# Down projections of a three-term float32r kernel: one 512-column product for the high weights instead of two of 256 columns

## The reference, cut to what matters

```python
# first block (tag f1 in the kernel), weights w_up / w_down
u = causal_depthwise_conv(h2 @ w_up[l], w_conv[l], b_conv[l])
val, gte = jnp.split(u, 2, axis=-1)
x = x + (1 + gate2[:, None, :]) * ((val * jax.nn.silu(gte)) @ w_down[l])
...
# second block, layer a (f2: a_gu / a_down) and layer b (f3: b_gu / b_down)
def swiglu(h, w_gu, w_down):
    gate, up = jnp.split(h @ w_gu, 2, axis=-1)
    return (jax.nn.silu(gate) * up) @ w_down
x = x + swiglu(rms_norm_2(x, a_norm2_g[i]), a_ffn_gu[i], a_ffn_down[i])
...
return rms_norm_2(x, final_norm_g)
```

## Time and profile before

| what | value |
|---|---|
| median of the three runs | 1055.43 us |
| lowest and highest | 1054.33 and 1056.28 us |
| span of the profiled execution | 1051.3 us |
| mean granted clock of TensorE in it | 0.997 of full speed |
| busy: PE, PEld, DVE, ACT | 97%, 92%, 70%, 53% |

### The profile page before, as it was taken

How to read it: one execution, slowest core, us unless ns; L and a number is a source line. 1 busy time by engine, 2 the same in 40 slices (tenths; PEclk the granted TensorE clock), 3 DMA queues, 4 the chain that set the end, 5 groups by cost and what they waited for, 6 DMA issues and landing times.

```text
span 1051.3 us, 22984 instructions
## 1 busy us (share of the span) xinstructions
PE 1020.2 (97%) x10004; PEld 966.9 (92%) x10004; DVE 733.6 (70%) x1194; ACT 562.0 (53%) x858; POOL 0.9 (0%) x7
## 2 busy tenths in 40 slices
PE   7999999999999999998999999999999999999996
PEld 6898889999999998986879999999888799999996
DVE  3898677899976667888557566566857665565654
ACT  4456474665565548764236444454667654444541
POOL 0000000000000000000000000000000000000000
PEclk9999999999999999999999999999999999999999
DMA  9978465466645553331005555465224435554541
GB/s 350 398 259 310 172 239 186 176 239 242 229 139 193 203 231 121 126 118 43 4 6 196 199 174 190 140 214 209 101 78 166 170 124 201 191 175 158 194 166 41
DMA packets 31236, 185.82 MB, mean 177 GB/s; under 512 B 3472, under 2 KB 4768, under 8 KB 13984
## 3 DMA queue, kind: packets, MB, share of 16 engines
q1 hardware_dynamic: 31136, 184.36, 49.2%
HBM read 183.29 MB, written 1.05 MB: 175 GB/s over the span
## 4 chain that ended last, share of the span: by engine, by line
PE 87%; DVE 5%; DMA 3%; ACT 3%; issue 1%; SPq 1%; DVEq 0%; ACTq 0%
PE banks L383 47%; PE banks L1390 17%; PE banks L348 3%; PE banks L380 2%; PE banks L660 1%; DMA land<-in_mkv_a 1%; DVE wlo L328 1%; PE banks L1933 1%; PE banks L1574 1%; PE banks L595 1%; PE banks L1923 1%; ACT whi L313 1%; PE banks L663 1%; DMA raw<-in_a_in 1%; DMA raw<-in_w_in 1%
## 5 line engine op out<-in xcount | busy, mean ns | idle before, releaser
L328 DVE TENSOR_TENSOR wlo<-raw,whi 128x2048 fp32r<-128x2048 f32 (+3 forms) x163 | 323.0, 1982 | 169.3 <-ACT whi L313 169.1
L313 ACT ACTIVATE whi<-raw 128x2048 fp32r<-128x2048 f32 (+3 forms) x163 | 270.7, 1663 | 107.4 <-PE banks L1390 73.5
L383 PE MATMUL banks<-h_lo,whi 128*128 128x256 f32 x1376 | 175.1, 279 | 0.0
L383 PE MATMUL banks<-h_hi,wlo 128*128 128x256 f32 x1376 | 173.1, 277 | 0.0
L383 PE MATMUL banks<-h_hi,whi 128*128 128x256 f32 x1360 | 172.1, 279 | 0.1
L383 PEld LDWEIGHTS banks<-h_lo,whi 128*128 128x128 f32 x1376 | 163.9, 187 | 3.2 <-issue 2.6
L383 PEld LDWEIGHTS banks<-h_hi,wlo 128*128 128x128 f32 x1376 | 163.8, 187 | 1.5 <-issue 1.2
L383 PEld LDWEIGHTS banks<-h_hi,whi 128*128 128x128 f32 x1360 | 162.1, 187 | 2.3 <-issue 1.2
L1416 ACT ACTIVATE u<-u 128x256 f32<-128x256 f32 x44 | 18.4, 418 | 124.9 <-DVE u L1470 124.9
L1390 PE MATMUL banks<-m_lo,whi 128*128 128x256 f32 x528 | 73.4, 278 | 0.0
L1390 PE MATMUL banks<-m_hi,wlo 128*128 128x256 f32 x528 | 73.2, 277 | 0.0
(11 more groups left out here) (453 smaller groups left out, 1408.8 us busy)
## 6 DMA issues: line engine op xcount, KB each, us to landing
raw<-in_ada SPq DMA_DIRECT2D x24, 1024.0 KB, 6.6
raw<-in_w_up SPq DMA_DIRECT2D x22, 1024.0 KB, 4.8
raw<-in_a_gu SPq DMA_DIRECT2D x22, 1024.0 KB, 4.8
raw<-in_b_gu SPq DMA_DIRECT2D x22, 1024.0 KB, 4.9
raw<-in_w_in SPq DMA_DIRECT2D x12, 1024.0 KB, 6.4
raw<-in_w_down SPq DMA_DIRECT2D x16, 704.0 KB, 4.1
raw<-in_a_in SPq DMA_DIRECT2D x11, 1024.0 KB, 6.3
raw<-in_a_down SPq DMA_DIRECT2D x16, 704.0 KB, 4.1
```

Source lines behind the costliest of these rows:

```text
L313: act.activation(hi_s[k % NSPLIT][:, 0:w], raw[n % NRAW][:, 0:w], ACT.Copy).then_inc(*hi_made.tick(k))
L328: dve.tensor_tensor(lo_s[s][:, 0:w], raw[n % NRAW][:, 0:w], hi_s[s][:, 0:w].bitcast(F), SUB).then_inc(*lo_made.tick(k))
L383: i_ = pe.matmul(b[0:m, j * T:(j + 1) * T], a[:, kt * step + j * m:kt * step + j * m + m], x[:, kt, :], start=st, stop=sp)
```

## The change

The gated values get one buffer `gated` of two halves, `m_hi` and `m_lo`, in place of two buffers. For f = 0 to 6 the terms with `whi` are no longer two matmuls of 256 columns: one matmul of 512 columns reads the `m_hi` and the `m_lo` tile of a block and writes both halves of the bank, one per input part. After each one follows the `wlo` matmul of 256 columns for the same block. So one f is 44 matmuls instead of 66, with the same 22 x 768 columns. For f = 7 the order and the shapes stay as they were. In the first half of f = 0 the matmul of a block now also waits for `m_lo`, and in the second half it waits for it two matmuls earlier than before. DVE has to add the second half of the bank: one more scalar_tensor_tensor per f in f1, a copy and an addition more per f in f2 and f3.

```diff
-        m_hi = sb("m_hi", [P, 22, T], R, s2)
-        m_lo = sb("m_lo", [P, 22, T], R, s2)
+        gated = sb("gated", [P, 2, 22, T], R, s2)
+        m_hi, m_lo = gated[:, 0, :, :], gated[:, 1, :, :]
...
-                    if f == 0 and half == 1:
-                        turns = [(n, kt) for kt in range(11) for n in range(3)]
+                    if f == 0:
+                        turns = [(n, kt) for kt in range(11) for n in range(2)]
+                    elif f < 7:
+                        turns = [(n, kt) for kt in range(11) for n in range(2)]
                     else:
                         turns = [(n, kt) for n in range(3) for kt in range(11)]
                     for o, (n, kt) in enumerate(turns):
-                        a, x = (lo if n == 1 else hi), (m_lo if n == 2 else m_hi)
+                        g = 11 * half + kt
+                        w = (lo if n == 1 else hi)[:, kt * P:kt * P + P]
                         if n == 1:
                             pe.wait_ge(*lo_made.at(k))
                         if f == 0 and n == 0:
-                            pe.wait_ge(*m_hi_a.at((tag, 11 * half + kt)))
-                        if f == 0 and n == 2:
-                            pe.wait_ge(*m_lo_v.at((tag, 11 * half + kt)))
+                            pe.wait_ge(*m_hi_a.at((tag, g)))
+                            pe.wait_ge(*m_lo_v.at((tag, g)))
                         last = o == len(turns) - 1
-                        x_ = pe.matmul(b[:, 0:T], a[:, kt * P:kt * P + P], x[:, 11 * half + kt, :],
-                                       start=half == 0 and o == 0, stop=half == 1 and last)
+                        st, sp = half == 0 and o == 0, half == 1 and last
+                        if f < 7 and n == 0:
+                            x_ = pe.matmul(v2(b), w, gated[:, :, g, :], start=st, stop=False)
+                        else:
+                            x_ = pe.matmul(b[:, 0:T], w, (m_lo if n == 2 else m_hi)[:, g, :], start=st, stop=sp)
...
                 if up == "w_up":
+                    if f < 7:
+                        dve.scalar_tensor_tensor(out=X[:, f, :], in0=b[:, T:2 * T], scalar=GATE2[:, f:f + 1],
+                                                 in1=X[:, f, :], op0=MUL, op1=ADD).then_inc(*ub_v.tick(key))
+                        dve.wait_ge(*ub_v.at(key))
...
-                    dve.tensor_tensor(ub[:, f, :], b[:, 0:T], rs_t[:, :], MUL).then_inc(*ub_v.tick(key))
+                    of = b[:, 0:T]
+                    if f < 7:
+                        of = ub[:, f, :]
+                        dve.tensor_copy(of, b[:, T:2 * T]).then_inc(*ub_v.tick((key, "low")))
+                        dve.wait_ge(*ub_v.at((key, "low")))
+                        dve.tensor_tensor(of, b[:, 0:T], of, ADD).then_inc(*ub_v.tick((key, "sum")))
+                        dve.wait_ge(*ub_v.at((key, "sum")))
+                    dve.tensor_tensor(ub[:, f, :], of, rs_t[:, :], MUL).then_inc(*ub_v.tick(key))
```

## The result

| | median us | lowest to highest | runs |
|---|---|---|---|
| before | 1055.43 | 1050.84 to 1057.73 | 9 |
| changed | 1060.08 | 1057.20 to 1062.33 | 9 |

The ratio is 1.0052, 95% interval 1.0037 to 1.0068 (it weighs the single runs and is not the quotient of the two medians, which is 1.0044): slower by about half a per cent, and the interval lies wholly above 1. 1055.9 us, no change to speak of, had been forecast.

A forecast was written before the change was run, and what follows sets the result against it. PE's matmul stream was taken to bound the kernel; terms of 0, +0.46 and 0 us on 1055.43 gave 1055.9 us. Its own range was 1055 to 1057, the wide range 1051.0 to 1060.5 us.

The forecast's parts named there:

- What bounds the kernel: Whole kernel: PE busy 97% at full clock; down-projection streams run at a quick 113.3 or slow 117.8 ns per 256-column product.
- term 1: Down projections, f = 0 to 6: a 512-column product costs 227 ns, like two of 256, so 462 fewer products save 0 us.
- The bounds of 227 to 241: Estimated ns for one 512-column float32r product in the down projections, from 0.443 to 0.47 ns per column.
- The removed weight loads: Down projections: dropping loads gives nothing, since 16-column weights show the same 113.8 ns pace, so the load was hidden.
- The 16-column rows: Profile rows of products with 16-column weights, 113.8 ns each, taken to show that pace doesn't depend on weight width.
- Term 2: PE's last block of f = 0 waits earlier for `m_lo`: +0.23 us in f2 and in f3, +0.46 us together.
- Term 3: DVE's added bank additions, 16 us in all over the three networks, hide behind PE: 0 us.
- Rival 1: Down projections: the excess is a price per product or load, so 462 fewer save 3.1 us, 1052.8; chance 0.22.
- Rival 2: f3's down projection falls into the quick pace and gives 2.05 us back, 1053.8; chance 0.16.
- Rival 3: Slow pace takes over at the first 512-column product after a wait: 1058.0 for one network, up to 1063.1; chance 0.30.
- the point of decision: Within rival 3: a cost of 4.6 ns per 512-column product (2.1 us / 462) decides the sign.

The follow-up runs named there:

- DVE's work alone: Kernel before with only the change's added DVE work, adding the bank's first half twice in f = 0 to 6: 1054.50 us against 1053.46, ratio 1.0000.
- the scan: Changed kernel, input parts side by side, f = 1 to 6 each running rows of another product width, down projection not computed: 1034.70 us, one run, only distances count.
- order alone: Kernel before with each block's three 256-column products following each other in f = 0 to 6, no 512-column product: 1053.40 us against 1053.46, ratio 1.0003.
- Everything but the width: Changed kernel with its 512-column product cut into two of 256, order, waits, bank halves and DVE additions kept: 1054.37 us against 1053.35, ratio 1.0008.

## Why the prediction was wrong, point by point

- **What bounds the kernel** was right: PE's stream, and inside it two paces at a full clock. f3's slow pace in the kernel before doesn't belong to f3: in the four other profiled kernels with 256-column products throughout the three networks it took 59.9 to 60.2 us, and two of them (DVE's work alone; the weight buffers moved) have PE's program unchanged. What picks the pace stays open.
- **The step that failed is term 1.** It put a 512-column product at 227 ns, "what 256 columns show twice over, since it is the pace measured longest". It is 233 to 235. The bounds of 227 to 241 from the 384-column rows were good, and these rows were the nearer ones: 384 columns took 176 and 177 ns in the later runs, which is 0.46 ns per column, 235 for 512. (Each of rows 5 is the second of a pair; the first starts 0.28 us before it, as the first of the scan's row of 384 columns does before the next. No run explains these 0.28 us, and a sum that took them in would have come out higher.) I took the lowest value of the range, from rows of the wrong width, over the middle of it from those nearer in width. Then, since the `wlo` product beside it is at its slow pace too, a block is 353.3 ns, 7 to 8 of the 13.3 ns from the 512 columns and the rest from the `wlo` product, so that the term is 154 x 13.3 = 2.05 us for a network that had been quick, and not 0. Measured: 2.01 us in f2, whose f = 7 stayed quick; 2.27 in f1, where f = 7 was slow as well (66 x 4.4 ns = 0.3 us); 0.24 in f3, which had been slow already.
- **The removed weight loads** were rightly priced at nothing. The reason was half right: at 256 columns and more the load is hidden, but at 256 only just (about 112 ns under 113). The 16-column rows show that 256 columns don't wait for it, not that it is short.
- **Term 2**, the earlier wait, had been put at 0.23 us a network: with order alone it was 0.17 in f2. In the changed kernel it is next to nothing. Its timeline at that place in f2, PE:

```profile
693.61 0.28 PE L1396 MATMUL banks<-gated,wlo 128*128 128x256 f32 x1
693.78 0.47 PE L1394 MATMUL banks<-gated,whi 128*128 128x512 f32 x1
694.09 0.28 PE L1396 MATMUL banks<-gated,wlo 128*128 128x256 f32 x1
```

  From 693.61 to 694.09 two products take 0.48 us instead of 0.35: a wait of 0.13 us, hardly more than the 0.1 before, and in f3 it is 0.1. That the slower stream arrives later at the last block would explain it, but it is argued. With the product cut in two ("Everything but the width"), the same waits and the quick stream, it was 0.1 us in f2 and 0.45 in f3, where the block before the last waited too, which the prediction had called safe.
- **Term 3**, DVE: nothing, as forecast; 14.5 busy us more in the three networks where 16 had been said.
- **The rivals.** Rival 1 (a price per product or per load) has fallen: by it fewer products would have saved 3.1 us. Rival 2, f3 back at the quick pace, was right about the kernel before, but the width holds f3 slow. Rival 3 came closest, with f1 and f2 both slow and the 512 near its upper bound, but its mechanism was another: no wait and no jump starts it, the width does, from the first block of every network. Its 4.6 ns per 512-column product as the point of decision was passed (6.7 to 8.3). The measured 1060.1 us lies just inside the range of 1051.0 to 1060.5; that is owed to the room left for rival 3, not to the sum.

## What to carry to other kernels

Don't merge two 256-column float32r products into one of 512 to save weight loads, where loads are hidden anyway: measure the wide form in a steady row first. When a price has to be taken from neighbours, the row nearest in the quantity that the change alters (here the width) counts more than the one with most repetitions. And compare stages by their stretches over several profiled executions before a stage's pace is called its own.

## What the runs showed that I had not expected

- A float32r product with a load of 128 weight columns of its own has a floor of about 110 to 112 ns, whatever its width up to 240 columns. From 272 columns on it costs 0.45 to 0.465 ns per column, more than the 0.42 of plain float32 if that takes two passes, as the prediction read it. Of the widths above the floor only 256 columns get to 0.443 (113.3 ns), with weights of 32 columns too, where the load is no floor. Why is open, and so is whether the excess belongs to float32r alone.
- Two paddings of 128 bytes between the weight buffers shift the pace of whole stretches of 256-column products, 288 of them from 32.80 to 33.92 us, others the opposite way; without them the kernel before is 0.66% slower (1.0042 to 1.0090) and its runs spread over 13 us instead of 5.
